# Decoder trunk on one core: conv taps on TensorE as three partial products of rounded operands, with a ring of 11 double tap matrices

## The chip, the cores and the metric

One core of one Trainium2 chip runs the whole program in one launch. The metric is the device time in microseconds (us); the host only lays data out. The engines are called as in the profile: PE is TensorE (its weight loads are listed as PEld), DVE is VectorE, ACT is ScalarE, POOL is GpSimd, SP issues the DMAs of the weights.

## What is computed

A trunk of two layers on 256 tokens of width 2048, all in float32. Layer 0 mixes with two convolution branches, layer 1 with attention; each layer then has an MLP and a gated embedding. The change touches only the first branch of layer 0:

```python
def conv_recurrent_mixer(hn, w_in, conv_a_w, conv_a_b, ln_a_g, ln_a_b, ...):
    u = hn @ w_in
    a_val, a_gate, xr, gr = jnp.split(u, [D_A, 2 * D_A, 2 * D_A + D_B], axis=-1)
    ya = a_val * jax.nn.sigmoid(a_gate)                      # GLU, 1024 channels
    ya = causal_depthwise_conv(ya, conv_a_w, conv_a_b)       # 31 taps for each channel
    ya = jax.nn.silu(layer_norm(ya, ln_a_g, ln_a_b))
    ...
    return jnp.concatenate([ya, yb], axis=-1) @ w_out
```

## The kernel before, in words

Every activation lies transposed in SBUF: 128 channels on the partitions, 256 tokens along the free dimension. A weight matrix comes in chunks of 512 rows by 256 columns, 812 chunks in all, through a ring of 4 raw buffers and a ring of 8 split buffers (`spl`). ACT rounds a chunk to fp32r (`split`, copy at L861), DVE or, for 12 chunks of this stretch (`SUMMED`), POOL subtracts the rounded part to get the remainder (L1337, L463), and PE multiplies three partial products: rounded by rounded, rounded by remainder, remainder by rounded. SP loads chunk m once the remainder of chunk m-4 is there; ACT splits chunk m once PE has used chunk m-8.

The GLU stretch has four pairs of channel tiles. Here chunk n means the n-th chunk from C_GLU on; pair c takes chunks 8c to 8c+3 for the values and 8c+4 to 8c+7 for the gates (`small_gemm`, L533 to L535, 24 matmuls for a chunk). After the last chunk of a pair DVE scales the gate (L1723), ACT takes its sigmoid (L1128), DVE multiplies (L1736, `glu_ready`).

The 31 taps of the convolution are shared out. Of the first tile of a pair DVE does 19 taps and POOL adds 12 products that ACT makes (`products`). Of the second tile PE does the first 14 taps (12 in the last pair) and DVE the rest. A tap on PE is one float32 matmul with a diagonal matrix of the tap's weights (L803); ACT makes the matrix from the identity (`tap_matrices`, L1174) in a ring of 22, `dg_ready` and `dg_used` counting both ways.

The order on each engine is written out by hand. On PE the taps of pair c-1 stand in three bursts (`conv`): 4 taps ahead of chunk 8c+6, 5 after chunk 8c+7, and 5 ahead of chunk 8c+10. The third burst of pair 2 comes ahead of chunk 33, where the output projection has begun with two chunks for a group, and the 12 taps of pair 3 come 3 at a time after chunks 33, 35, 37 and 39. ACT goes through `glu_pair(c)`: eight turns q, each with an eighth of the tap matrices of pair c-1, the split of chunk 8c+8+q and, from q=1 to 6, two products; then the sigmoid of pair c. At q=4 of c=1 it also rounds a tile XB of 2048 columns. So all matrices of pair c-1 are made ahead of the sigmoid of pair c. DVE goes through its own `glu_pair(c)`: taps in eight parts, remainders, `glu_value` and `conv_end(c-2)` at q=3, and at the end the gate and the multiplication. `conv_end` adds the parts of PE (L1810), DVE and POOL, and sums tiles for the layer norm; PE's `ln_mean` (L818) ahead of chunk 41 waits for the last of these sums.

Of the kernel before, what the change touches and what calls it, by code (L numbers as in the profile page):

```python
# [28 lines left out]
P = 128  # L29
D = 2048  # L30
T = 256
# [38 lines left out]
NDG = 22  # L70
# [28 lines left out]
LAM_STEPS = 17  # L99
OUT_PIECES = ((0, 2), (2, 6), (6, 11), (11, 16))  # L100
# [28 lines left out]
def trunk(nc, xT, pT, par, w_in, w_rg_a, w_rg_x, w_out, w_qkv, w_o, w_up, w_down, w_proj, w_gate, outT):  # L129
    with ExitStack() as ctx:  # L130
# [29 lines left out]
        with nc.sbuf_tensor("glu", [P, 8, PAD_A + T], F32) as glu, \  # L160
                nc.sbuf_tensor("xrp", [P, 2, XRP], F32) as xrp, \
                nc.sbuf_tensor("rest", [P, 8 * 2 * T - 8 * (PAD_A + T) - 2 * XRP], F32) as rest, \
                nc.sbuf_tensor("rg", [P, 8, 2, T], F32) as rg:
            prod = rest[:, 0:NPROD * T].rearrange("p (k n) -> p k n", k=NPROD)
# [6 lines left out]
        pp = sb("pp", [P, NT, T])  # L171

# [6 lines left out]
        with nc.sbuf_tensor("y", [P, 8, T], F32) as y, nc.sbuf_tensor("y2", [P, T], F32) as y2, \  # L179
                nc.sbuf_tensor("dg", [P, NDG, P], F32) as dg, nc.sbuf_tensor("ident", [P, P], F32) as ident:  # L180
            pass
# [57 lines left out]
        ln_sum = sem("ln_sum")  # L239
        dg_ready = sem("dg_ready")  # L240
        dg_used = sem("dg_used")
        conv_taken = sem("conv_taken")
        xr_step = sem("xr_step")
# [60 lines left out]
        def par_col(c):  # L304
            return params[:, bass.ds(c, 1)]

# [133 lines left out]
        def _(pool):  # L440
# [4 lines left out]
            pool.memset(glu[:, :, 0:PAD_A], 0.0)  # L445
            pool.memset(xrp[:, :, 0:PAD_B], 0.0)
# [38 lines left out]
        def _(pe):  # L485
# [304 lines left out]
            def conv(pair, part, parts):  # L790
# [4 lines left out]
                if part == 0:  # L795
                    pe.wait_ge(glu_ready, pair + 1)
# [3 lines left out]
                for k in range(part * n // parts, (part + 1) * n // parts):  # L800
                    tap = taps_upto(pair) + k
                    pe.wait_ge(dg_ready, tap + 1)
                    pe.matmul(O[:, pair % 2, 0:256], dg[:, tap % NDG, :], glu[:, bass.ds(pair * 2 + 1, 1), k:k + T],  # L803
                              start=(k == 0), stop=(k == n - 1), skip_group_check=True).then_inc(dg_used, 1)
# [54 lines left out]
        def _(act):  # L859
# [187 lines left out]
            act.wait_ge(par_rest, 16)  # L1047
            act.activation(small[:, 0, :], params[:, LAMBDA:LAMBDA + 8], ACT.Abs).then_inc(lam_abs, 1)
# [117 lines left out]
            def tap_matrices(pair, part, parts):  # L1166


                n = TAPS_PE[pair]
                for k in range(part * n // parts, (part + 1) * n // parts):  # L1170
                    tap = taps_upto(pair) + k
                    if tap >= NDG:
                        act.wait_ge(dg_used, tap + 1 - NDG)
                    act.activation(dg[:, tap % NDG, :], ident[:, :], ACT.Copy,  # L1174
                                   scale=par_col((pair * 2 + 1) * CA + (CONV_A_W + k))).then_inc(dg_ready, 1)
# [12 lines left out]
            def glu_pair(c):  # L1188
                for q in range(8):
                    tap_matrices(c - 1, q, 8)  # L1190
# [7 lines left out]
                glu_gate(c)  # L1198

            act.wait_ge(rg_vec, 11)  # L1200
# [24 lines left out]
            for s in range(NG):  # L1225
                if s < 4:
# [793 lines left out]
```

## Time and profile before

| | us |
|---|---|
| median of 3 runs | 2348.19 |
| lowest, highest | 2347.66, 2349.77 |
| the profiled execution, its time | 2347.8 |
| its span, first to last instruction | 2346.1 |
| busy in the span: PE, DVE, ACT, POOL | 2324.9, 1534.6, 1252.6, 77.1 |

The page gives busy time for each engine and the chain of work that ended last. The trace behind it is asked by stretch of time, by line or tile, or as a timeline. The GLU stretch runs from about 105 us to 220 us of the span, the taps on PE from 145 us to 243 us. In a timeline the duration of a matmul reaches beyond the start of the next; the distance between starts is what a matmul costs in a stream. The same holds for ACT and DVE, whose instructions overlap by about 0.1 us.

### The profile page before, as it was taken

How to read it: one execution, taken by the hardware profiler on the slowest of the kernel's cores; microseconds unless marked ns; L12 is line 12 of the kernel's file. 1: busy time of each engine (PE TensorE's matmuls, PEld its weight loads, DVE VectorE, ACT ScalarE, POOL GpSimd, SP SyncE). 2: the span in 40 equal slices, each digit the busy share in tenths (PEclk: the TensorE clock that was granted, in tenths of full speed). 3: DMA queues.
4: the chain of work that ended last, by engine and by line, in shares of the span. 5: the costliest groups of instructions: out<-in, count | busy, mean ns of one | idle time of the engine just before them, and what ended most of it. 6: DMA issues, size and time to landing. Idle time of an engine off the chain costs nothing.

```text
span 2346.1 us, 39851 instructions
## 1 busy us (share of the span) xinstructions
PE 2324.9 (99%) x13964; PEld 2078.5 (89%) x13964; DVE 1534.6 (65%) x1848; ACT 1252.6 (53%) x1616; POOL 77.1 (3%) x73
## 2 busy tenths in 40 slices
PE   8999999999999999999999999999999999999998
PEld 7999998888888888888888888888888888888887
DVE  8899776556556555668676666765555555556666
ACT  6876655445445435556666666555444444445454
POOL 0046100000000000000000000000000000000000
PEclk9999999999999999999999999999999999999999
DMA  8555465655655665665555555565556556556553
GB/s 254 181 181 161 154 206 172 195 179 190 194 189 182 191 199 179 188 205 174 186 179 157 176 170 177 180 190 179 189 196 188 180 194 198 179 184 202 186 166 122
DMA packets 432334, 431.24 MB, mean 184 GB/s; under 512 B 13312, under 2 KB 430208, under 8 KB 432256
## 3 DMA queue, kind: packets, MB, share of 16 engines
q1 hardware_dynamic: 431968, 429.97, 58.1%
q8 instruction: 49, 0.80, 0.1%
q10 hardware_dynamic: 288, 0.23, 0.0%
q14 instruction: 29, 0.24, 0.0%
HBM read 428.05 MB, written 2.10 MB: 183 GB/s over the span
## 4 chain that ended last, share of the span: by engine, by line
PE 97%; DVE 1%; ACT 1%; DMA 1%; issue 0%; DVEq 0%; ACTq 0%; SPq 0%
PE ps L492 54%; PE ps L498 28%; PE ps L533 3%; PE ps L534 3%; PE ps L535 3%; PE ps L490 2%; PE ps L497 1%; PE O L803 1%; DVE spl L1337 1%; DMA raw<-in_w_o 0%; PE O L654 0%; PE Z L628 0%; ACT spl L861 0%; PE Z L637 0%; PE ps L707 0%
## 5 line engine op out<-in xcount | busy, mean ns | idle before, releaser
L1337 DVE TENSOR_TENSOR spl<-raw,spl 128x1024 fp32r<-128x1024 f32 x797 | 938.6, 1222 | 579.5 <-ACT spl L861 572.2
L861 ACT ACTIVATE spl<-raw 128x1024 fp32r<-128x1024 f32 (+1 forms) x811 | 817.3, 1054 | 686.5 <-PE ps L498 593.7
L492 PE MATMUL ps<-XA,spl 128*128 128x512 f32 x2816 | 705.0, 392 | 7.3 <-DVE spl L1545 6.7
L492 PE MATMUL ps<-XB,spl 128*128 128x512 f32 x2784 | 711.5, 392 | 0.0
L492 PEld LDWEIGHTS ps<-XA,spl 128*128 128x128 f32 x2816 | 505.1, 189 | 91.5 <-issue 7.4
L492 PEld LDWEIGHTS ps<-XB,spl 128*128 128x128 f32 x2784 | 491.4, 188 | 75.6
L498 PEld LDWEIGHTS ps<-XB,spl 128*128 128x128 f32 x2784 | 394.5, 191 | 39.0
L498 PEld LDWEIGHTS ps<-XA,spl 128*128 128x128 f32 x2816 | 387.3, 191 | 31.4
L498 PE MATMUL ps<-XB,spl 128*128 128x256 f32 x2784 | 402.6, 281 | 0.0
L498 PE MATMUL ps<-XA,spl 128*128 128x256 f32 x2816 | 393.8, 282 | 0.0
L1373 DVE TENSOR_TENSOR tv<-cross,ps 128x512 f32<-128x512 f32 x181 | 123.2, 681 | 13.2 <-ACT cross L861 13.0
L941 ACT ACTIVATE tv<-tv 128x512 f32<-128x512 f32 x64 | 40.5, 633 | 168.8 <-DVE tv L1428 168.8
L861 ACT ACTIVATE cross<-ps 128x512 f32<-128x512 f32 (+1 forms) x184 | 106.4, 578 | 12.1 <-PE ps L498 11.9
L490 PE MATMUL ps<-spl,XB 128*128 128x512 f32 x256 | 80.7, 397 | 0.0
L533 PE MATMUL ps<-XB,spl 128*128 128x256 f32 x256 | 73.9, 289 | 0.0
L533 PE MATMUL ps<-XA,spl 128*128 128x256 f32 x256 | 73.7, 288 | 0.0
L534 PE MATMUL ps<-XA,spl 128*128 128x256 f32 x256 | 72.4, 283 | 0.0
L535 PE MATMUL ps<-XA,spl 128*128 128x256 f32 x256 | 72.4, 283 | 0.0
L534 PE MATMUL ps<-XB,spl 128*128 128x256 f32 x256 | 72.4, 283 | 0.0
L535 PE MATMUL ps<-XB,spl 128*128 128x256 f32 x256 | 72.4, 283 | 0.0
L1415 DVE TENSOR_TENSOR h<-h,tv 128x512 f32 (+1 forms) x87 | 60.3, 693 | 12.6 <-DVE tv L1373 11.3
L914 ACT ACTIVATE tv<-h 128x512 f32 (+1 forms) x47 | 29.7, 631 | 60.5 <-DVE h L1415 58.7
(207 smaller groups left out, 1531.6 us busy)
## 6 DMA issues: line engine op xcount, KB each, us to landing
raw<-in_w_up SPq DMA_DIRECT2D x256, 512.0 KB, 4.8
raw<-in_w_down SPq DMA_DIRECT2D x256, 512.0 KB, 5.2
raw<-in_w_qkv SPq DMA_DIRECT2D x96, 512.0 KB, 4.4
raw<-in_w_gate SPq DMA_DIRECT2D x64, 512.0 KB, 4.6
raw<-in_w_in SPq DMA_DIRECT2D x63, 512.0 KB, 4.7
raw<-in_w_out SPq DMA_DIRECT2D x32, 512.0 KB, 3.6
raw<-in_w_o SPq DMA_DIRECT2D x32, 512.0 KB, 4.8
raw<-in_w_proj SPq DMA_DIRECT2D x8, 512.0 KB, 4.1
```

The source lines that it names most:

```text
L490: pe.matmul(ps[:, b + o, :], x[:, kt, 0, c], w[:, q, :, :], start=start, stop=False)
L492: pe.matmul(ps[:, b + o, :], w[:, q, 0, c], x[:, kt, :, :], start=start, stop=False)
L498: return pe.matmul(ps[:, b + o, 0:256], w[:, q, 1, c], x[:, kt, 0, :], start=False, stop=stop)
L533: pe.matmul(out, w[0], x[0], start=start, stop=False, skip_group_check=True)
L534: pe.matmul(out, w[0], x[1], start=False, stop=False, skip_group_check=True)
L535: return pe.matmul(out, w[1], x[0], start=False, stop=stop, skip_group_check=True)
L861: return act.activation(out, in_, ACT.Copy, scale=scale)
L914: act.activation(tv[:, :, :], h[:, bass.ds(t0, 2), :], ACT.Square).then_inc(sq_ready, 1)
L941: act.activation(tv[:, :, :], tv[:, :, :], ACT.Square).then_inc(up_sq, 1)
L1337: dve.tensor_tensor(s[:, :, 1, :], raw[:, m % NRAW, :, :], s[:, :, 0, :].bitcast(F32), ALU.subtract).then_inc(lo_ready, 1)
L1373: dve.tensor_tensor(tv[:, :, :] if out is None else out, cross[:, :, :], ps[:, b:b + 2, 0:256], ALU.add).then_inc(sum_ready, 1)
L1415: dve.tensor_tensor(ht, ht, tv[:, :, :], ALU.add).then_inc(res_ready, 1)
```

## The change

The second tile of each GLU pair and its tap weights are rounded to fp32r and their remainders kept (`gs`, `wt`). A tap on PE becomes two fp32r matmuls in place of one float32 matmul: the rounded weights times rounded tile and remainder together (512 columns), and the weights' remainder times the rounded tile (256 columns). Two matrices are made for a tap, the ring holds 11 such pairs in the memory of the former 22, and ACT's order of making them changes. `round_glu` is new on ACT after each sigmoid, a subtraction is new on DVE after each multiplication, and `conv_end` has one addition more. The products of ACT for POOL move from `rest` to a part of `pp`.

```diff
-NDG = 22
+NDG = 11
...
+                nc.sbuf_tensor("gs", [P, 2, 2, PAD_A + T], F32R) as gs, \
+                nc.sbuf_tensor("wt", [P, 2, 4, NWT], F32R) as wt, \
...
+            pool.memset(gs[:, :, :, 0:PAD_A].bitcast(F32), 0.0)
...
                 if part == 0:
-                    pe.wait_ge(glu_ready, pair + 1)
+                    pe.wait_ge(gs_ready, pair + 1)
...
                     pe.wait_ge(dg_ready, tap + 1)
-                    pe.matmul(O[:, pair % 2, 0:256], dg[:, tap % NDG, :], glu[:, bass.ds(pair * 2 + 1, 1), k:k + T],
-                              start=(k == 0), stop=(k == n - 1), skip_group_check=True).then_inc(dg_used, 1)
+                    w = dg[:, tap % NDG, :, :]
+                    pe.matmul(O[:, pair % 2, :], w[:, 0, :], gs[:, pair % 2, :, k:k + T],
+                              start=(k == 0), stop=False, skip_group_check=True)
+                    pe.matmul(O[:, pair % 2, 0:256], w[:, 1, :], gs[:, pair % 2, 0, k:k + T],
+                              start=False, stop=(k == n - 1), skip_group_check=True).then_inc(dg_used, 1)
...
+            copy(wt[:, 0, :, :], taps_of_pe()).then_inc(wt_hi, 1)
...
-            def tap_matrices(pair, part, parts):
-
-
-                n = TAPS_PE[pair]
-                for k in range(part * n // parts, (part + 1) * n // parts):
+            def tap_matrices(pair, k0, k1):
+
+
+                for k in range(k0, k1):
                     tap = taps_upto(pair) + k
                     if tap >= NDG:
                         act.wait_ge(dg_used, tap + 1 - NDG)
-                    act.activation(dg[:, tap % NDG, :], ident[:, :], ACT.Copy,
-                                   scale=par_col((pair * 2 + 1) * CA + (CONV_A_W + k))).then_inc(dg_ready, 1)
+                    for j in range(2):
+                        r = act.activation(dg[:, tap % NDG, j, :], ident[:, :], ACT.Copy,
+                                           scale=wt[:, j, pair, k:k + 1].bitcast(F32))
+                    r.then_inc(dg_ready, 1)
+
+            def round_glu(pair):
+
+                if pair >= 2:
+                    act.wait_ge(conv_taken, pair - 1)
+                act.wait_ge(glu_ready, pair + 1)
+                copy(gs[:, pair % 2, 0, PAD_A:], glu[:, 2 * pair + 1, PAD_A:]).then_inc(gs_hi, 1)
...
             def glu_pair(c):
                 for q in range(8):
-                    tap_matrices(c - 1, q, 8)
+                    if q < 2 and c >= 2:
+                        tap_matrices(c - 2, TAPS_PE[c - 2] * (4 + q) // 6, TAPS_PE[c - 2] * (5 + q) // 6)
+                    elif q >= 2:
+                        n = TAPS_PE[c - 1]
+                        cut = (0, 0, 0, n // 12, n // 6, n // 4, n // 3, n // 2, 2 * n // 3)
+                        tap_matrices(c - 1, cut[q], cut[q + 1])
                     split(C_GLU + NSPL + 8 * c + q)
...
                 glu_gate(c)
-
-            act.wait_ge(rg_vec, 11)
+                round_glu(c)
+
+            act.wait_ge(rg_vec, 12)
+            act.wait_ge(wt_ready, 1)
+            round_glu(0)
             glu_pair(1)
...
             for s in range(NG):
+                if s == 0:
+                    tap_matrices(2, TAPS_PE[2] * 4 // 6, TAPS_PE[2])
                 if s < 4:
-                    tap_matrices(3, s, 4)
+                    tap_matrices(3, s * TAPS_PE[3] // 4, (s + 1) * TAPS_PE[3] // 4)
...
+            dve.wait_ge(wt_hi, 1)
+            dve.tensor_tensor(wt[:, 1, :, :], taps_of_pe(), wt[:, 0, :, :].bitcast(F32),
+                              ALU.subtract).then_inc(wt_ready, 1)
...
                 dve.wait_ge(glu_ready, c + 1)
+                dve.wait_ge(gs_hi, c + 1)
+                dve.tensor_tensor(gs[:, c % 2, 1, PAD_A:], glu[:, 2 * c + 1, PAD_A:],
+                                  gs[:, c % 2, 0, PAD_A:].bitcast(F32), ALU.subtract).then_inc(gs_ready, 1)
...
-                dve.tensor_tensor(second, second, O[:, pair % 2, 0:256], ALU.add).then_inc(conv_taken, 1)
+                for j in range(2):
+                    dve.tensor_tensor(second, second, O[:, pair % 2, j * T:(j + 1) * T], ALU.add).then_inc(
+                        (conv_half, conv_taken)[j], 1)
+                    if j == 0:
+                        dve.wait_ge(conv_half, pair + 1)
```

## Rows read from the trace of the kernel before

**Rows 1.** The page: busy time of PE, and the chain that ended last by engine

```profile
PE 2324.9 (99%) x13964; PEld 2078.5 (89%) x13964; DVE 1534.6 (65%) x1848; ACT 1252.6 (53%) x1616; POOL 77.1 (3%) x73
...
PE 97%; DVE 1%; ACT 1%; DMA 1%; issue 0%; DVEq 0%; ACTq 0%; SPq 0%
```

**Rows 2.** Stretches: length; busy us of PE, PEld, DVE, ACT, POOL; PEclk; DMA share; GB/s

```profile
138.00:163.00 25.00, 25.00 (x188) 24.25 (x188) 24.24 (x44) 19.37 (x36) 19.91 (x14) 1.00 0.68 209
...
214.00:248.00 34.00, 32.31 (x244) 31.19 (x242) 31.42 (x62) 18.36 (x34) 17.45 (x14) 1.00 0.48 147
```

**Rows 3.** Timeline of PE at two bursts: start, duration, engine, line, operation

```profile
145.01 0.28 PE L535 MATMUL ps<-XA,spl 128*128 128x256 f32 x1
145.13 1.89 PE L803 MATMUL O<-glu,dg 128*128 128x256 f32 x8
146.67 0.47 PE L533 MATMUL ps<-XA,spl 128*128 128x256 f32 x1
146.98 0.28 PE L534 MATMUL ps<-XA,spl 128*128 128x256 f32 x1
...
160.54 2.33 PE L803 MATMUL O<-glu,dg 128*128 128x256 f32 x10
```

**Rows 4.** Timeline of PE in the projection before the GLU stretch

```profile
101.28 0.63 PE L492 MATMUL ps<-XA,spl 128*128 128x512 f32 x2
101.74 0.40 PE L498 MATMUL ps<-XA,spl 128*128 128x256 f32 x2
101.97 0.63 PE L492 MATMUL ps<-XA,spl 128*128 128x512 f32 x2
```

**Rows 5.** Timeline of ACT in turns of c=1, and the sigmoid that ends them

```profile
137.81 1.06 ACT L861 ACTIVATE spl<-raw 128x1024 fp32r<-128x1024 f32 x1 [0.89 <-DMA raw<-in_w_in]
...
142.50 0.68 ACT L1174 ACTIVATE dg<-ident,params 128x128 f32<-128x128 f32 x2
143.08 1.04 ACT L861 ACTIVATE spl<-raw 128x1024 fp32r<-128x1024 f32 x1
144.03 0.89 ACT L861 ACTIVATE rest<-glu,params 128x256 f32<-128x256 f32 x2
...
149.27 1.90 ACT L861 ACTIVATE XB<-pp 128x2048 fp32r<-128x2048 f32 x1
...
165.28 0.63 ACT L1128 ACTIVATE tv<-tv 128x512 f32<-128x512 f32 x1 [7.91 <-DVE tv L1723]
```

**Rows 6.** Timeline of DVE at the multiplications of pairs 0 and 1

```profile
136.00 0.69 DVE L1736 TENSOR_TENSOR glu<-glu,tv 128x512 f32<-128x512 f32 x1 [0.35 <-ACT tv L1128]
...
138.90 1.22 DVE L1337 TENSOR_TENSOR spl<-raw,spl 128x1024 fp32r<-128x1024 f32 x1 [0.65 <-ACT spl L861]
...
164.56 0.68 DVE L1723 TENSOR_TENSOR tv<-ps,rB 128x512 f32<-128x512 f32 x1
166.01 0.69 DVE L1736 TENSOR_TENSOR glu<-glu,tv 128x512 f32<-128x512 f32 x1 [0.77 <-ACT tv L1128]
```

**Rows 7.** The tile `raw` from 125 to 165 us: from issue to landing

```profile
DMA to landing us min/median/max: 3.7/4.8/6.6
```

**Rows 8.** Waits from 246 to 300 us: total, times, longest

```profile
PE Z L818 <- DVE nacc L1818: 1.7, 1, 1.7
```

**Rows 9.** Stretches at the end of the span, columns as in rows 2

```profile
2334.00:2338.00 4.00, 1.38 (x8) 1.04 (x8) 1.98 (x6) 1.71 (x4) 0.00 (x0) 0.84 0.00 0
2338.00:2346.00 8.00, 0.00 (x0) 0.00 (x0) 3.66 (x3) 0.00 (x0) 0.00 (x0) 0.50 0.77 262
```

**Rows 10.** Timeline of PE at the end of its work

```profile
2332.48 0.51 PE L717 MATMUL Z<-onesD,nacc 128*128 128x1 f32 x4
2334.99 0.61 PE L721 MATMUL Z<-onesD,tv 128*128 128x1 f32 x4 [2.00 <-DVE tv L1523]
```

**Rows 11.** Timeline of PE near the start of the span

```profile
10.65 1.05 PE L492 MATMUL ps<-XA,spl 128*128 128x512 f32 x2
...
11.94 0.76 PE L492 MATMUL ps<-XA,spl 128*128 128x512 f32 x2
```

More of the change, by code:

```diff
@@ L99 @@
 LAM_STEPS = 17
+NWT = 18
+assert 8 * 2 * T == 8 * (PAD_A + T) + 2 * XRP + 4 * (PAD_A + T) + 8 * NWT
 OUT_PIECES = ((0, 2), (2, 6), (6, 11), (11, 16))
@@ L161, in trunk @@
                 nc.sbuf_tensor("xrp", [P, 2, XRP], F32) as xrp, \
-                nc.sbuf_tensor("rest", [P, 8 * 2 * T - 8 * (PAD_A + T) - 2 * XRP], F32) as rest, \
+                nc.sbuf_tensor("gs", [P, 2, 2, PAD_A + T], F32R) as gs, \
+                nc.sbuf_tensor("wt", [P, 2, 4, NWT], F32R) as wt, \
                 nc.sbuf_tensor("rg", [P, 8, 2, T], F32) as rg:
-            prod = rest[:, 0:NPROD * T].rearrange("p (k n) -> p k n", k=NPROD)
+            pass
         XB = sb("XB", [P, NT, 2, T], F32R)
@@ L171, in trunk @@
         pp = sb("pp", [P, NT, T])
+        prod = pp[:, 8:8 + NPROD, :]
         with nc.sbuf_tensor("wrg", [P, 2, 4, 2, 256], F32R) as wrg:
@@ L179, in trunk @@
         with nc.sbuf_tensor("y", [P, 8, T], F32) as y, nc.sbuf_tensor("y2", [P, T], F32) as y2, \
-                nc.sbuf_tensor("dg", [P, NDG, P], F32) as dg, nc.sbuf_tensor("ident", [P, P], F32) as ident:
+                nc.sbuf_tensor("dg", [P, NDG, 2, P], F32R) as dg, nc.sbuf_tensor("ident", [P, P], F32) as ident:
             pass
@@ L239, in trunk @@
         ln_sum = sem("ln_sum")
+        wt_hi = sem("wt_hi")
+        wt_ready = sem("wt_ready")
+        gs_hi = sem("gs_hi")
+        gs_ready = sem("gs_ready")
         dg_ready = sem("dg_ready")
@@ L242, in trunk @@
         conv_taken = sem("conv_taken")
+        conv_half = sem("conv_half")
         xr_step = sem("xr_step")
@@ L305, in par_col, with taps_of_pe @@
             return params[:, bass.ds(c, 1)]
+        def taps_of_pe():
+            return params[:, CONV_A_W:CONV_A_W + 8 * CA].rearrange("p (c j k) -> p c j k", c=4, j=2)[:, :, 1, 0:NWT]
         def gain(n, t):
```

## The prediction

> **What bounds the kernel now.** I read the page first: PE is busy for 99% of the span and 97% of the chain [rows 1]. Second, the busy time by stretch: in the GLU stretch PE is busy throughout until 214 us, DVE too is busy for 97% (24.24 of 25.00), and ACT for 77%, before it gets new work [rows 2]. Third, the timelines of PE, ACT and DVE side by side. PE sets the end, so PE time saved or lost here reaches the end in full; DVE has almost no room, and it decides when ACT may take the sigmoid of a pair: ACT waited 7.91 us for it at c=1 [rows 5]. The last question is whether each matrix is ready when its burst begins. Before, all of them were made ahead of that sigmoid. The change puts 5 of 14 behind it.
>
> **What a tap costs on PE.** Old: between the last matmul ahead of the first burst (145.01) and the second behind it (146.98) lie 1.97 us, of which two ordinary steps are 0.24; 1.73 for 4 taps is 0.43 a tap [rows 3]. New: two matmuls of 512 and two of 256 columns took 101.97 - 101.28 = 0.69 us, so one of each 0.35 [rows 4]. 54 taps save 54 x 0.08 = 4.5 us on PE. Bounds: a spacing of 0.12 for each 256 columns, as in small_gemm (the two steps above), gives 0.36 and 3.8 us; for the other end I take 0.34 and 4.9.
>
> **What is added to ACT and DVE.** Two matrices in a row take 143.08 - 142.50 = 0.58 us, so each of 54 new ones 0.29, 15.7 us in all; a pair of products, 256 columns each, is 0.8 by starts, so round_glu is 0.45; a split 0.95 to 1.0 [rows 5]. A pair of 14 taps gives ACT 4.1 us more in some 28 us of PE, so ACT isn't overloaded. DVE gets per pair a 256-column subtraction and an addition, about 0.4 us each, and a wait for ACT's rounding. The memset of pads on POOL (0.2 us), the rounding of the tap weights on ACT and their subtraction on DVE (0.2 us each, at 25 us and later) lie beside PE's work, and before the start of the first products on POOL; if that cover were gone they would cost their 0.6 us. The products' new place costs the same. No DMA is added; but loads go out when DVE has a remainder, so DVE's delay moves SP's queue.
>
> **First stall: ahead of chunk 14.** ACT must round the GLU tile behind the split of chunk 15 (137.81 [rows 5]), so at 138.8 to 139.2, and DVE, which has multiplied by 136.7, stands until 139.3, subtracts to 139.7, and only then makes the remainders of chunks 14 and 15. Queued behind its wait are these, the taps, and with them the loads of chunks 18 and 19. The second (begun at 138.90, 1.14 by starts [rows 6]) ended at 140.0, now at 142.0: DVE is 2.0 us late. So chunk 18 is loaded from 140.9 and, by 4.5 to 4.8 us to landing [rows 7], there at 145.4; 19 at 146.9, 20 at 149.3. ACT then goes: split 16 and 17 and two products by 142.5, matrices of tap 0 by 143.1; waits for chunk 18, split 146.4, products 147.2, tap 1 by 147.8; split 19, products, tap 2 by 150.2; split 20 151.1, products 151.9, XB 153.7 (1.8 us, [rows 5]), tap 3 by 154.3. PE comes at 145.13 [rows 3] and finds tap 0; without a wait it would be done at 146.5, now at 154.7. That is 8.2 us. The old order had made the fourth matrix by 143.1.
>
> **Second stall: ahead of chunk 18.** PE: chunks 14 and 15 (24 x 0.12 = 2.88 us each) to 160.4, second burst 162.2 (tap 8 is made by 160.9), chunks 16 and 17 to 168.0. DVE: 2.0 us late, waits about 0.7 for the split of chunk 22 (ACT has three taps' matrices to make ahead of it), so its gate begins at 167.2 - 0.7 = 166.6, where it was 164.56, and the product is there at 168.75 (it was 166.70) [rows 6]. ACT: rounding to 169.25, taps 9 and 10 to 170.4, split 171.4, taps 11 to 13 to 173.1. PE ends this burst at 173.4 instead of 169.7: 3.7 us. Even with DVE no later than before it would be 166.7 + 0.5 + 1.2 + 1.0 + 1.75 + 0.35 = 171.5, where the burst that began at 160.54 [rows 3] ended at 162.7. That floor does not depend on the first stall.
>
> **Third and fourth.** From here ACT and DVE go in step with PE, which frees the chunks. Let T be the end of chunk 22. ACT has split chunk 30 at T + 1.0; DVE's remainder (1.1), its six taps (2.5), the remainder of chunk 31 (1.2) and the gate (0.7) end at T + 6.6, sigmoid T + 7.3, product T + 8.1, rounding T + 8.6, and the last of the five pairs of matrices with a split between, T + 12.5, the burst T + 12.85. PE alone would end it at T + 2.9 + 1.75 + 5.8 + 1.75 = T + 12.1: 0.7 us, I take 0.6. For pair 2 one chunk less lies in front of the burst and no split between the matrices: T + 11.8 against T + 9.25, 2.55 us. The taps of pair 3 are made in time (ahead of chunk 34 by 230.9, needed at 232.4). Then DVE waits for the split of chunk 40, which stands behind 8 pairs of matrices (4.6 us), and comes to ln_mean 3.0 us after PE, where PE had waited 1.8 (1.7 in the waits [rows 8], and 0.1 of reentry): +1.2.
>
> **The clock.** At the end of the span PE had only a few tiny matmuls from 2332.48 on and waited 2.00 us ahead of those at 2334.99 [rows 10]; the granted clock was 0.84 of 2.4 GHz in the mean of 2334 to 2338 and 0.50, the 1.2 GHz level, after it [rows 9]. In the first stall PE would run two taps, 0.7 us, in 8.8 us, much the same. I take it that the clock falls once. At the start a set of two 512 and two 256 columns took 11.94 - 10.65 = 1.29 us [rows 11], at full clock 0.69 [rows 4], and this lasted from 6.7 to 11.9: 5.3 us at half speed, a loss of 2.65. It passes through, since ACT and DVE wait for PE's chunk 14: +2.65. The Trainium skill, page "TensorE: Matmul & The Clock Gate", Part 1, says that the array falls to half clock when idle and must be kept at work for a while before it is given the full clock again, and warns against idle gaps; by it this is a cost of the change, and if it didn't hold in a gap broken by single taps, my sum would be 11.9 (the second rival).
>
> **Sum.** 8.2 + 3.7 + 0.6 + 2.55 + 1.2 + 2.65 - 4.5 = 14.4 us. The profiled execution took 2347.8 with a span of 2346.1, so 2360.5 of span and 2362.2; the median is 0.4 above that execution: 2362.6.
>
> **The rivals.**
> 1. The forecast, 2362.6. For it: the order of ACT's queue is fixed, and DVE was too late for it by 5 us before (sigmoid 165.28 against a burst at 160.54 [rows 3, 5]). Chance 0.48.
> 2. The same stalls, but the clock stays: 14.4 - 2.65, 2360.0. For it: single taps in the gap, and the first stall may be shorter if loads land at the 3.7 end [rows 7]. Chance 0.20.
> 3. ACT and DVE are less late: DVE finds its 2 us again by 164 us, the first stall is 5 us with the clock kept, and ln_mean's wait doesn't grow. Since the second stall makes up for a shorter first one, what counts is the gate: 11.75 - 2.0 - 0.7 - 1.2 = some 8, 2356. Chance 0.16.
> 4. The clock falls again, in the second stall (1.4 us idle, then one and two taps at a time) or in the fourth: 2.65 more, 2365.3. Chance 0.08.
> 5. Faster: the matrices are ready for every burst and only PE's 4.5 us count, 2343.7. It decides at one place, the matrices of taps 9 to 13 of each pair: the gate of pair 1 would have to be ready about 10 us earlier than 166.70 [rows 6], which would need DVE to run its taps in less than half the time. Its weakness is that nothing in the change takes work from DVE. Chance 0.04.
> 6. The change doesn't do what it says: matmuls on gs and dg go at the rate of float32. Then a tap costs 3 x 0.43 = 1.3 us and 54 of them 51 us more than forecast, 2414. Against it: the same type and form go at 0.35 in [rows 4]. Chance 0.02, and 0.02 for what I haven't seen.
>
> The range of 8 in 10 leaves out 4 to 6 in part: from 2355.0, rival 3 with its own play of 1 us, to 2366.5, rival 4 and a first stall 1.2 us longer. A measurement of this kernel can tell about 0.2%, 4.7 us, from no change. Faster by more than that 0.03, within it 0.05 (the edge of 5 and the best of 3), slower 0.92.
>
> **What would show it.** Right: the waits of PE name ACT's `dg` (its L1174), some 12 to 15 us in about four groups, the largest ahead of chunk 14 and ending with tap 3, just after XB's rounding; each third burst ends right after the five pairs of matrices which follow round_glu; the matmuls of taps have starts 0.35 us apart for a tap; the clock has a stretch at half speed after the first gap and PE is less than 98% busy in 145 to 235 us. Wrong: PE has no waits at bursts (then 5), a tap of more than 0.4 us (then part of the saving is gone), no fall of the clock (2), or waits at the second bursts, which I take to be in time by 0.5 us or more except the first. Outside the stretch from 138 to 262 us nothing should move but the time at which it happens.

## The result, and the profile after

| | before | after |
|---|---|---|
| median, us | 2348.98 of 6 runs | 2366.71 of 6 runs |
| lowest to highest, us | 2347.66 to 2351.10 | 2365.88 to 2369.19 |
| profiled execution, its span, us | 2347.8, 2346.1 | 2369.19, 2367.5 |

The change makes the kernel slower by 17.7 us: 1.0076 of the time before, 95% interval 1.0065 to 1.0088. The forecast was 2362.6 us with 2355.0 to 2366.5; the direction is right, the median lies 0.2 us above the range. The profiled execution of after is the longest of its six, 2.5 us above their median, and that of before lies 1.2 us under its median, so the two spans differ by 21.4 us, 3.7 more than the medians.

The page of after, busy time and the chain that ended last by engine, which answers to [rows 1]:

```profile
PE 2331.0 (98%) x13964; PEld 2080.4 (88%) x13964; DVE 1539.9 (65%) x1857; ACT 1271.7 (54%) x1675; POOL 75.0 (3%) x74
...
PE 89%; DVE 7%; ACT 2%; DMA 1%; issue 1%; SPq 0%; DVEq 0%; ACTq 0%
```

The chain now runs for 7% through DVE. The waits of after from 138 to 290 us (who waited <- for whom: us in total, times, longest):

```profile
PEld O L818 <- ACT dg L1192: 16.5, 14, 3.9
ACT tv L1146 <- DVE tv L1762: 12.5, 3, 7.3
PE O L818 <- ACT dg L1192: 12.3, 7, 3.5
...
DVE gs L1778 <- ACT gs L878: 3.4, 4, 1.6
...
PE Z L835 <- DVE nacc L1864: 2.4, 1, 2.4
```

PE waits for ACT's tap matrices, which it did not do at all before. ACT itself was never idle ahead of one of its 108 matrices, so none of them waited for a free place in the ring. The first burst on PE, which answers to the taps of [rows 3] (start, duration, then in brackets the idle time before it and what ended it):

```profile
148.49 0.40 PE L818 MATMUL O<-gs,dg 128*128 128x512 f32 x1
148.72 0.28 PE L820 MATMUL O<-gs,dg 128*128 128x256 f32 x1
149.83 0.50 PE L818 MATMUL O<-gs,dg 128*128 128x512 f32 x1 [0.83 <-ACT dg L1192]
...
152.16 0.60 PE L818 MATMUL O<-gs,dg 128*128 128x512 f32 x1 [1.71 <-ACT dg L1192]
...
156.36 0.79 PE L818 MATMUL O<-gs,dg 128*128 128x512 f32 x1 [3.39 <-ACT dg L1192]
156.95 0.41 PE L820 MATMUL O<-gs,dg 128*128 128x256 f32 x1
```

Each tap comes alone, with a growing gap ahead of it; the fourth starts 7.9 us after the first. ACT in the same stretch, and up to the second stall:

```profile
153.83 1.89 ACT L878 ACTIVATE XB<-pp 128x2048 fp32r<-128x2048 f32 x1
155.63 0.68 ACT L1192 ACTIVATE dg<-ident,wt 128x128 fp32r<-128x128 f32 x2
...
172.46 0.63 ACT L1146 ACTIVATE tv<-tv 128x512 f32<-128x512 f32 x1 [7.27 <-DVE tv L1762]
173.92 0.42 ACT L878 ACTIVATE gs<-glu 128x256 fp32r<-128x256 f32 x1 [0.83 <-DVE glu L1775]
174.24 1.26 ACT L1192 ACTIVATE dg<-ident,wt 128x128 fp32r<-128x128 f32 x4
175.41 1.04 ACT L878 ACTIVATE spl<-raw 128x1024 fp32r<-128x1024 f32 x1
176.36 1.84 ACT L1192 ACTIVATE dg<-ident,wt 128x128 fp32r<-128x128 f32 x6
```

Tap 3's pair of matrices comes right behind XB. The sigmoid waited 7.27 us for DVE's gate (7.91 before [rows 5]), and only behind it and the rounding of the tile are the matrices of taps 9 to 13 made. PE's third burst, which stands for them:

```profile
174.97 0.50 PE L818 MATMUL O<-gs,dg 128*128 128x512 f32 x1 [3.47 <-ACT dg L1192]
...
177.09 0.79 PE L818 MATMUL O<-gs,dg 128*128 128x512 f32 x1 [0.92 <-ACT dg L1192]
```

A burst of pair 1 that finds its matrices ready shows the price of a tap (last and first matmuls of the chunks around the five taps):

```profile
199.47 0.28 PE L549 MATMUL ps<-XA,spl 128*128 128x256 f32 x1
199.59 0.40 PE L818 MATMUL O<-gs,dg 128*128 128x512 f32 x1
...
201.36 0.28 PE L547 MATMUL ps<-XA,spl 128*128 128x256 f32 x1
201.47 0.28 PE L548 MATMUL ps<-XA,spl 128*128 128x256 f32 x1
```

From 199.47 to 201.47 lie 2.00 us; less two ordinary steps of 0.12, five taps took 1.76, 0.352 a tap. Last, the granted clock. The columns are the stretch and its length, busy us (instructions) of PE, PEld, DVE, ACT and POOL, the clock as a share of 2.4 GHz, the DMA share and GB/s:

```profile
145.00:152.00 7.00, 4.62 (x35) 3.98 (x33) 6.96 (x14) 5.65 (x14) 6.45 (x5) 1.00 0.83 259
152.00:159.00 7.00, 3.45 (x13) 2.85 (x14) 6.93 (x11) 7.00 (x14) 6.57 (x6) 0.53 0.56 184
159.00:176.00 17.00, 13.53 (x103) 12.67 (x101) 15.61 (x26) 7.50 (x18) 4.77 (x5) 0.99 0.39 124
176.00:183.00 7.00, 6.08 (x26) 5.62 (x25) 5.45 (x12) 4.53 (x12) 3.07 (x2) 0.52 0.29 79
183.00:268.00 85.00, 80.55 (x616) 76.59 (x616) 73.42 (x147) 62.36 (x139) 50.40 (x40) 1.00 0.46 143
268.00:272.00 4.00, 4.00 (x21) 3.95 (x21) 3.00 (x2) 0.97 (x1) 0.00 (x0) 0.57 0.46 128
```

Three stretches are at the 1.2 GHz level: one in the first stall, one right behind the second, and one behind the wait at `ln_mean`. Ahead of each PE had just stood with no or hardly any matmuls.

**Where the time went.** For every matmul which both kernels have outside the taps I took its start in after less its start in before. I call the shift just ahead of the first burst the head. It is 3.4 us here (0.7 from 9 us of the span on, 2.9 from 60, 3.3 from 103). In a second profiled execution of the same kernel (`ctl_after`, below) it is 0.8, and in the other kernels 0.5 to 2.4, so it is a variation of the start and not the change. The growth of the shift behind the head, cleared of the 0.08 us that each tap saves:

| place | summed as | after | `ctl_after` |
|---|---|---|---|
| first stall | 8.2 | 7.4 | 8.55 |
| clock, first fall | 2.65 | 0.75 | 1.5 |
| second stall | 3.7 | 6.25 | 4.35 |
| clock, second fall | none | 1.5 | 1.35 |
| third burst of pair 1 | 0.6 | 1.0 | 1.0 |
| third burst of pair 2 | 2.55 | 2.95 | 2.95 |
| `ln_mean` | 1.2 | 0.75 | 0.75 |
| clock, third fall | none | 1.45 | 1.5 |
| saving on 54 taps | -4.5 | -4.3 | -4.3 |
| sum | 14.4 | 17.8 | 17.7 |

The first three lines measure 14.4 together in both executions, though each line differs between them, and were summed as 14.55. The excess is in the falls of the clock that were not in the sum, 2.95 us, and in two stalls of 0.4 us more each, less 0.45 at `ln_mean`.

### The profile page after: what moved, and what is told of

Same layout as the page of the kernel before. It is cut to its first block, busy times and chain, and to the rows that moved or that the text cites. A ratio compares the mean times of both kernels' runs of the same rounds, so it can differ in the third digit from the quotient of the medians.

```text
span 2367.5 us, 39923 instructions
## 1 busy us (share of the span) xinstructions
PE 2331.0 (98%) x13964; PEld 2080.4 (88%) x13964; DVE 1539.9 (65%) x1857; ACT 1271.7 (54%) x1675; POOL 75.0 (3%) x74
## 4 chain that ended last, share of the span: by engine, by line
PE 89%; DVE 7%; ACT 2%; DMA 1%; issue 1%; SPq 0%; DVEq 0%; ACTq 0%
PE ps L506 51%; PE ps L512 27%; PE ps L504 2%; DVE spl L1373 2%; PE ps L547 2%; PE ps L549 2%; PE ps L548 2%; DMA raw<-in_w_in 1%; PE ps L511 1%; ACT spl L878 1%; DVE Z L1823 1%; DVE Z L1835 1%; PE O L668 0%; DVE pp L1621 0%; PE Z L642 0%
## 5 line engine op out<-in xcount | busy, mean ns | idle before, releaser
L512 PEld LDWEIGHTS ps<-XA,spl 128*128 128x128 f32 x2816 | 387.3, 191 | 31.4
```

What stands on the lines that cost most here:

```text
L512: return pe.matmul(ps[:, b + o, 0:256], w[:, q, 1, c], x[:, kt, 0, :], start=False, stop=stop)
```

## The experiments

The kernel before was timed on the same chip beside every one; its medians lie between 2348.7 and 2349.4 us. Ratios are to it, with 95% intervals.

A trace is one execution, and not always a typical one. So that traces can be compared, the table has for each kernel the head and what the stretch from there to 275 us lost against before. The last two columns are the starts of DVE's product in pairs 1 and 3, less the head (before: 166.0 and 217.0). All in us.

| kernel | median | the profiled one | head | lost in the stretch | product 1 | product 3 |
|---|---|---|---|---|---|---|
| after | 2366.71 | 2369.19 | 3.4 | 17.9 | 169.8 | 229.9 |
| `ctl_after` | 2368.57 | 2367.14 | 0.8 | 17.7 | 169.8 | 229.7 |
| `xb_later` | 2367.44 | 2367.99 | 2.2 | 18.0 | 170.5 | 229.2 |
| `f32_new_order` | 2357.22 | 2356.70 | 0.6 | 8.1 | 167.3 | 223.5 |
| `ring14b_old` | 2357.57 | 2358.15 | 1.4 | 8.9 | 169.3 | 223.7 |
| `f32_rounding` | 2355.03 | 2356.57 | 1.3 | 7.2 | 171.2 | 223.7 |
| `pool_no_rest` | 2367.79 | 2368.94 | 2.2 | 18.9 | 170.9 | 231.0 |
| `xb_later_no_rest` | 2364.81 | 2367.02 | 1.6 | 17.0 | 169.0 | 229.1 |
| `f32_rounding_no_rest` | 2352.46 | 2354.05 | 1.8 | 3.2 | 167.5 | 220.2 |
| `before_no_rest` | 2350.09 | 2350.58 | 2.0 | 0.0 | 165.3 | 217.4 |
| `f32_rounding_defer` | 2354.50 | 2353.62 | 1.4 | 4.4 | 169.7 | 222.0 |
| `ring14_defer` | 2357.44 | 2354.42 | 0.9 | 5.7 | 168.2 | 222.7 |
| `light_dve` | 2355.94 | 2354.90 | 2.4 | 3.9 | 167.8 | 221.3 |
| `more_taps` | 2356.33 | 2356.61 | 1.3 | 7.4 | 169.6 | 223.8 |
| `fillers` | 2365.01 | 2364.77 | 0.5 | 15.7 | 171.1 | 229.2 |

**1. The changed kernel again, `ctl_after`.** No edit: is what the profile of after shows the rule?

> The changed kernel once more, unchanged, as the base of the other runs. In its first profile PE came to the first burst 3.36 us later than before, most of it from loads that landed late in the first 60 us, and lost 18.0 us between there and 272 us. Theory: the 3.4 us is variation of the start and is mostly absent here, so 2366.5 (2365.5 to 2368), with the 18 us of the stretch again within 0.5. Rival: the head start is lost by the change itself, then PE again arrives at about 148.5.

2368.57 us of 4 runs, 1.0086 (1.0069 to 1.0102). Its first burst starts at 145.97, 2.5 us earlier than in the profile of after, with the same waits, and its clock is at half from 149.4 to 159.6, 173.3 to 180.1 and 265.5 to 268.9. So the three falls belong to the change, and the late start of that other execution doesn't.

**2. Shorten the first stall alone, `xb_later`.** In the first stall ACT rounds XB ahead of tap 3; one turn later it is out of the way.

```diff
-                    if c == 1 and q == 4:
+                    if c == 1 and q == 5:
```

> The change, with ACT's rounding of the 2048 columns of XB at turn 5 of c=1 in place of turn 4, so behind the matrices of tap 3. The first burst ends 1.8 us earlier. Theory (the gate sets the end of the third burst): the second stall grows by as much, total 2366.5 to 2367, no more than 0.5 us gained. Rival (stalls add up): 1.8 us faster and one fall of the clock less, 2363.5.

2367.44 us of 4 runs, 1.0078 (1.0061 to 1.0095). The first burst ran from 147.34 to 154.84, 7.5 us where it took 8.7 in after and 9.8 in its repeat. The product of pair 1, DVE's L1775, came no earlier (172.74; less the head 170.5 against 169.8), and the third burst ended at 178.7, 31.4 us after the first began (30.7 in after and in its repeat). What the first stall gave, the second took: the third burst stands behind the gate. Here the clock fell a fourth time, at 234.0 to 237.5, so how often it falls is itself not fixed.

**3. Only the order, `f32_new_order`.** The kernel before, its matmuls in float32 and single matrices, with ACT's new order and 11 places in the ring.

```diff
-NDG = 22
+NDG = 11
...
-                    tap_matrices(c - 1, q, 8)
+                    if q < 2 and c >= 2:
+                        tap_matrices(c - 2, TAPS_PE[c - 2] * (4 + q) // 6, TAPS_PE[c - 2] * (5 + q) // 6)
+                    elif q >= 2:
...
+                        tap_matrices(c - 1, cut[q], cut[q + 1])
```

> The kernel before with one part of the change alone: the float32 taps and single matrices stay, no rounding, but the ring has 11 slots and ACT makes the matrices in the order of the change. Theory (the order is the cost): taps 9 to 13 stand behind the sigmoid, whose product is at 166.7, so the third burst of pair 0 ends near 169.6 in place of 162.7, and for the later pairs some 1.3 us and one fall of the clock are added: 2348.7 + 7 to 10, 2356 to 2359. Rival (the double matrices, the rounding and DVE's wait are the cost): within 2 us of before.

2357.22 us of 6 runs, 1.0032 (1.0020 to 1.0044): 8 us for the order, with the ring of 11 that goes with it. Its waits name the same pair of engines:

```profile
ACT tv L1128 <- DVE tv L1729: 11.2, 3, 5.4
...
PE O L803 <- ACT dg L1173: 4.7, 3, 3.1
```

The time is as expected and its place is not. PE's shift grew by 5.4 us at the first burst, by 1.9 at half clock behind it (150.3 to 157.1), and by only 0.5 and 0.3 at third bursts. The expectation had put nearly all of it at the third burst of pair 0, behind the sigmoid; there PE came late already. The trace does not tell which of the two places would be enough by itself. The size of the ring changed too. Here as well ACT was never idle ahead of a matrix (54 of them), which speaks against it as a cause. The kernel that would divide order and size, 14 places with the change's order (`ring14`), gave no time, nor did a first form of the next one (`ring14_old`).

**4. Everything but the order, `ring14b_old`.** The change with 14 pairs of matrices, three of them in the unused end of `pp`, so that ACT's old order is possible.

```diff
-NDG = 11
+NDG = 14
...
-                    if q < 2 and c >= 2:
-                        tap_matrices(c - 2, TAPS_PE[c - 2] * (4 + q) // 6, TAPS_PE[c - 2] * (5 + q) // 6)
-                    elif q >= 2:
...
+                    tap_matrices(c - 1, q * n // 8, (q + 1) * n // 8)
```

> Ring of 14 double matrices (three slots in free tiles of pp), and ACT's order of before: an eighth of a pair's matrices ahead of each split, all 14 ahead of the sigmoid. Theory (order): the second, third and fourth stall go (5.9, 0.6 and 2.6 us net of savings), the clock doesn't fall there, and about 1 us of stall is left in the second burst of pair 0 behind the rounding of XB; DVE is still late at the layer norm. 2345 to 2349. Rival (ACT and DVE have too little room for 54 more matrices and the rounding, whatever the order): 2356 or more.

2357.57 us of 6 runs, 1.0034 (1.0021 to 1.0046). I had expected the gain to appear, and it did not: 9 of the 18 us went with the order, 8 stayed. The large stalls are gone. At 218 us PE is 0.8 us behind before, with a head of 1.4: of the 3.4 us that 42 taps save 0.6 is left in hand, and small waits at the bursts took the rest. Then, ahead of the first tap of pair 3:

```profile
227.05 0.77 PE L826 MATMUL O<-gs,dg 128*128 128x512 f32 x1 [5.25 <-ACT dg L1200]
```

The waits call the weight load beside it `PEld O L826 <- DVE gs L1780: 5.4, 1, 5.4`: it is the remainder of the last GLU tile. The clock went to half behind that gap, too:

```profile
214.00:224.00 10.00, 7.62 (x55) 6.68 (x54) 9.97 (x20) 5.20 (x13) 7.19 (x6) 1.00 0.53 157
224.00:231.00 7.00, 3.95 (x15) 3.69 (x16) 5.10 (x11) 5.72 (x14) 0.88 (x1) 0.51 0.24 77
```

DVE is busy for 9.97 of 10.00 us ahead of it, and its delay takes back more than PE had in hand. In PE's shift this wait makes 6.3 us and the half clock behind it 0.65. The longer wait at `ln_mean` (3.4 us, 1.7 before [rows 8]) makes 1.7, and another fall of the clock behind that (258.3 to 261.7) 1.5.

**5. Only the rounding, `f32_rounding`.** The kernel before with ACT's rounding of the GLU tile, DVE's wait and subtraction, and the products in `pp`; PE goes on with the float32 tile.

```diff
+                act.wait_ge(glu_ready, pair + 1)
+                copy(gs[:, pair % 2, 0, PAD_A:], glu[:, 2 * pair + 1, PAD_A:]).then_inc(gs_hi, 1)
...
+                dve.wait_ge(gs_hi, c + 1)
+                dve.tensor_tensor(gs[:, c % 2, 1, PAD_A:], glu[:, 2 * c + 1, PAD_A:],
+                                  gs[:, c % 2, 0, PAD_A:].bitcast(F32), ALU.subtract).then_inc(gs_ready, 1)
```

> The kernel before with another part of the change alone: ACT rounds the second GLU tile after each sigmoid and DVE waits for it and subtracts, but nothing reads the result; the taps stay float32 matmuls, with the single matrices, ring and order of before. Theory (DVE has no room in this stretch, so its added wait and work reach the end through the gate of the last pair and the layer norm): DVE is late by 2 us at pair 0 and by about 0.9 us more for each pair, minus what it waited before; 2351 to 2356, shown as waits ahead of the taps of pair 3 or the mean. Rival (DVE's additions lie beside PE's work): within 1.5 us of before.

2355.03 us of 10 runs, 1.0025 (1.0015 to 1.0034): 6 us for two instructions and a wait a pair. Again the last pair pays; of the 7.2 us that this trace lost, 5.0 are the wait ahead of pair 3's taps and 1.4 the half clock behind it (225.5 to 232.3):

```profile
ACT tv L1132 <- DVE tv L1736: 25.9, 3, 10.5
...
PEld O L807 <- DVE glu L1749: 3.8, 1, 3.8
```

The start of DVE's product in each pair, here with the head in it, shows where it falls behind (us; the spacing is the time DVE takes for a pair):

| kernel | pair 0 | 1 | 2 | 3 | spacings |
|---|---|---|---|---|---|
| before | 136.00 | 166.01 | 191.03 | 216.95 | 30.0, 25.0, 25.9 |
| f32_rounding | 137.71 | 172.51 | 198.32 | 225.09 | 34.8, 25.8, 26.8 |
| ring14b_old | 137.30 | 170.65 | 197.41 | 225.12 | 33.4, 26.8, 27.7 |
| after | 139.79 | 173.19 | 204.28 | 233.26 | 33.4, 31.1, 29.0 |

The later spacings grow by 0.8 and 0.9 in `f32_rounding`, about what the wait for ACT's rounding (0.55 and 0.6 us) and the subtraction (0.4) cost. The first grows by 4.8, more than the one wait and the one subtraction in it can make (2.0 us and 0.4).

**6. What stretches the first spacing: POOL.** In after, DVE's remainders of one chunk, and POOL's:

```profile
146.10 2.16 DVE L1373 TENSOR_TENSOR spl<-raw,spl 128x1024 fp32r<-128x1024 f32 x1
...
152.10 2.22 DVE L1373 TENSOR_TENSOR spl<-raw,spl 128x1024 fp32r<-128x1024 f32 x1
...
157.84 3.12 DVE L1373 TENSOR_TENSOR spl<-raw,spl 128x1024 fp32r<-128x1024 f32 x1
164.80 1.21 DVE L1373 TENSOR_TENSOR spl<-raw,spl 128x1024 fp32r<-128x1024 f32 x1
```

```profile
144.76 2.41 POOL L477 TENSOR_TENSOR spl<-raw,spl 128x1024 fp32r<-128x1024 f32 x1 [141.88 <-ACT spl L878]
...
150.87 2.37 POOL L477 TENSOR_TENSOR spl<-raw,spl 128x1024 fp32r<-128x1024 f32 x1 [0.26 <-ACT spl L878]
...
157.48 2.39 POOL L477 TENSOR_TENSOR spl<-raw,spl 128x1024 fp32r<-128x1024 f32 x1
```

A subtraction that starts on DVE while POOL's is under way overlaps it by 1.07, 1.14 and 2.03 us, and is longer than 1.22 by 0.94, 1.0 and 1.9. Four kernels test what that costs. In all of them POOL leaves out its 12 remainders and only marks the chunk as done, which takes a part of the computation away. The chunk is also marked earlier, so SP may load the next one sooner: the edit takes away the clash, and a little more.

```diff
-                pool.tensor_tensor(w[:, :, 1, :], raw[:, m % NRAW, :, :], w[:, :, 0, :].bitcast(F32),
-                                   ALU.subtract).then_inc(lo_summed[m % NSPL], 16)
+                pool.memset(w[:, 0, 1, 0:1].bitcast(F32), 0.0).then_inc(lo_summed[m % NSPL], 16)
```

After with this edit, `pool_no_rest`:

> The change, but POOL doesn't subtract the remainders of its 12 chunks; it clears one column and signals. The remainders of these chunks are left out. Theory (DVE and POOL share a way to SBUF): DVE's remainders at 146.10, 152.10 and 157.84, which took 2.16, 2.22 and 3.12 us while POOL subtracted, take 1.22 again, the gate of pair 1 comes 2 to 3.8 us earlier, and the second stall shrinks by as much: 2362.5 to 2365. Rival (DVE is slow there for another reason, its reading of tiles that ACT just wrote): the three stay above 2 us and the time stays at 2366.7 to 2368.

2367.79 us of 4 runs, 1.0074 (1.0058 to 1.0089): nothing. Up to pair 1's product all remainders of DVE took 1.21 to 1.23 us, and yet the product stayed at 173.15 (less the head 170.9, in after 169.8). DVE and ACT of this kernel say why:

```profile
164.19 1.23 DVE L1372 TENSOR_TENSOR spl<-raw,spl 128x1024 fp32r<-128x1024 f32 x1 [4.06 <-ACT spl L877]
```

```profile
163.09 1.06 ACT L877 ACTIVATE spl<-raw 128x1024 fp32r<-128x1024 f32 x1 [2.55 <-PE ps L548]
```

DVE, now early, waits for a split; the split waits for PE to free a buffer, and PE is late from its own first stall, which with the half clock behind it took 10.9 us of PE's shift here (7.9 in after, 9.8 in its repeat). My reading was that two ways of nearly equal length lead to the gate. If so, both must be shortened. After with this edit and that of `xb_later` together, `xb_later_no_rest`:

> Both edits together that gained nothing alone: XB rounded behind tap 3's matrices, and POOL leaving out its 12 remainders. Theory (two ways lead to the gate of pair 1, one through DVE's slowed remainders, one through PE's late chunk 14, ACT's split of chunk 22 and DVE's wait for it, nearly equally long): only with both shortened the gate comes earlier, by 1.5 to 2.5 us, 2363 to 2366. Rival (neither matters): 2366.7 to 2368.

2364.81 us of 4 runs, 1.0065 (1.0049 to 1.0080). Its four runs, 2363.0 to 2367.0, lie mostly below the ten of the changed kernel, 2365.9 to 2369.2, but the intervals overlap. The product of pair 1 is at 170.67, less the head 169.0: 1.5 and 1.9 us earlier than with one edit alone, but only 0.8 earlier than in after and its repeat, where 1.5 to 2.5 had been expected. The stretch lost 17.0 us against 17.9 and 17.7. So both edits together give somewhat more than either alone, as two ways to one gate would have it, but less than 1 us in the trace; the reading is supported and not shown. Next the same edit in `f32_rounding`, where no stall of PE stands beside it, `f32_rounding_no_rest`:

> f32_rounding without POOL's 12 remainders, which are left out (one column is cleared instead). In f32_rounding three remainders of DVE took 3.22, 1.97 and 3.30 us in place of 1.22, 4.8 in all, in before one took 1.95. Theory (the clash of DVE and POOL is the larger part of the loss): the products of pairs 0 and 1 stand 30.5 to 31.5 us apart in place of 34.8, and the time falls by 3 to 5 us, 2350 to 2352. Rival: no gain, 2354 to 2356.

2352.46 us of 10 runs, 1.0012 (1.0003 to 1.0022), 2.6 us under `f32_rounding`; the first spacing is 30.7. The base to which this belongs is the kernel before without POOL's remainders, `before_no_rest`:

> The base of the run above: the kernel before without POOL's 12 remainders, which are left out. Theory: DVE loses only 0.7 us to the clash there, and PE waited 1.7 for the layer norm's mean, so 0.5 to 1.5 us faster than before, 2347.5 to 2348.5. Rival (POOL costs DVE more than its lengthened instructions show): 3 us or more faster.

2350.09 us of 10 runs, 1.0003 (0.9994 to 1.0012): no gain, with spacings of 29.1, 25.0 and 27.0. I read it so that before, DVE had room for the clash, and with the added work it hasn't. So of the 6 us that the rounding costs, 2.6 go with POOL's remainders. Without them it still costs 2.4 (2352.5 against 2350.1). The trace of `f32_rounding_no_rest`, 1.6 us above its median, has 3.2 of this kind: 0.75 at the second burst of pair 0, 0.4 at chunk 33, 0.5 at `ln_mean`, and 1.5 at half clock behind that (251.4 to 254.8).

**7. DVE's wait out of the way, `f32_rounding_defer` and `ring14_defer`.** DVE stands for ACT's rounding ahead of two remainders, and with them two loads. Here its wait and subtraction of pairs 0 to 2 come behind the next pair's taps, where ACT is done.

```diff
+            def rest_of_glu(c):
+                dve.wait_ge(gs_hi, c + 1)
+                dve.tensor_tensor(gs[:, c % 2, 1, PAD_A:], glu[:, 2 * c + 1, PAD_A:],
+                                  gs[:, c % 2, 0, PAD_A:].bitcast(F32), ALU.subtract).then_inc(gs_ready, 1)
...
+                if q == 1 and pair < 3:
+                    rest_of_glu(pair)
```

> f32_rounding (float32 taps, rounding of the GLU tile added, result unused) with DVE's subtraction for pairs 0 to 2 moved behind its next split and the taps of the first turn, so that DVE doesn't stand still for ACT's rounding. Theory (DVE's lateness at pair 3's gate is the cost, and its largest parts are the wait of 2 us at pair 0 and the clash with POOL that this brings): 3 to 5 us faster than f32_rounding, 2350 to 2352.5. Rival (the added operations as such): no more than 1 us faster, 2354 to 2356.

2354.50 us of 8 runs, 1.0025 (1.0014 to 1.0035): no difference that can be told from 2355.03. The first spacing is still 33.3, with remainders of 1.95 and 3.13 us; pair 3's product came 1.7 us earlier than in `f32_rounding`, less the heads. The same in `ring14b_old`:

> ring14b_old (all of the change's arithmetic, ring of 14, order of before) with DVE's subtraction moved as in f32_rounding_defer. Theory: the wait ahead of the first taps of pair 3 (5.4 us there) shrinks to 1 to 3, the clock stays up, 2352 to 2354.5; still slower than before, since DVE has 3 to 4 us more to do and PE's saving can't reach past the mean of the layer norm. Rival (the double matrices on ACT delay DVE): 2356 or more.

2357.44 us of 6 runs, 1.0032 (1.0020 to 1.0045), against 2357.57. PE was ahead of before by 0.66 us at chunk 33, although its head was 0.95 late, and then stood 5.4 us for the remainder of pair 3 (`PEld O L826 <- DVE gs L1773: 5.4, 1, 5.4`). This trace is the fastest of its six runs, 3.0 us under their median, and here too the product came 1.0 us earlier. My theory that the wait ahead of the remainders is the main cost falls with these two runs: moving it brought the last product 1.0 to 1.7 us forward and the median nowhere.

**8. Take work from DVE, `light_dve` and `more_taps`.** `ring14b_old` with the remainder of the GLU tile on POOL and the three products of a tap as three matmuls of 256 columns into one half, which spares `conv_end` its second addition.

```diff
+                if n % 3 == 0:
+                    c = n // 3
+                    pool.wait_ge(gs_hi, c + 1)
+                    pool.tensor_tensor(gs[:, c % 2, 1, PAD_A:], glu[:, 2 * c + 1, PAD_A:],
+                                       gs[:, c % 2, 0, PAD_A:].bitcast(F32), ALU.subtract).then_inc(gs_ready, 1)
...
+                    for a, b in ((0, 0), (0, 1), (1, 0)):
+                        mm = pe.matmul(O[:, pair % 2, 0:256], tap_slot(tap, a), gs[:, pair % 2, b, k:k + T],
```

> All of the change's arithmetic, with ring of 14 and the order of before, and DVE's work put back to that of before: POOL subtracts the remainder of the rounded GLU tile, and a tap is three matmuls of 256 columns into one half, so conv_end has one addition. Theory (DVE sets the time at which the layer norm's mean can be taken, and PE waited 1.7 us for it before): PE's savings of 3.8 us turn into a longer wait there, 2347.5 to 2350, equal to before. Rival (PE's saving reaches the end): 2344 to 2346.

2355.94 us of 6 runs, 1.0031 (1.0019 to 1.0044), where a time equal to that of before was expected. By chunk 33 PE had gained 2.4 us on its head, and then:

```profile
PEld O L832 <- POOL gs L487: 4.8, 1, 4.8
```

Pair 3's product came at 223.68, less the head 4.3 us later than before, where `ring14b_old` was 6.8 later. So DVE's added tile work is a part of its delay, but not all. `more_taps` also gives PE two more taps of each pair and so takes them from DVE:

```diff
-TAPS_PE = (14, 14, 14, 12)
+TAPS_PE = (16, 16, 16, 14)
```

> light_dve with 2 more taps of each pair on PE in place of DVE (16, 16, 16, 14). PE gets 8 x 0.36 = 2.9 us more, DVE 8 x 0.39 = 3.1 us less, ACT 16 matrices more. Theory (DVE bound): 3 us faster than light_dve, 2345 to 2347, faster than before. Rival (PE bound): 1 to 3 us slower than light_dve.

2356.33 us of 7 runs, 1.0031 (1.0020 to 1.0042). Eight taps fewer on DVE did not bring pair 3's product forward (225.06; less the head 2.5 us later than in `light_dve`). From 136 us to 226 us DVE waits 6.7 us in 7 places for ACT's splits (3.3 in 5 in `light_dve`, 1.0 in 2 before), so I take it that ACT, with two matrices for each tap, had become the later one; that is argued and no run divides it. What the two runs show is that no price of DVE's tile work alone explains its delay.

**9. Fill the gaps, `fillers`.** The changed kernel with matmuls whose products are thrown away or add nothing in PE's gaps: 5, 12 and 25 ahead of taps 1, 2 and 3, 25 and 5 ahead of taps 9 and 11, and 16 at `ln_mean`.

```diff
+                    for _ in range(FILL.get(tap, 0)):
+                        pe.matmul(O[:, pair % 2, 0:256], gs[:, pair % 2, 0, 0:1].broadcast_to([P, P]),
+                                  gs[:, pair % 2, 0, k:k + T], start=False, stop=False, skip_group_check=True)
```

> The change, with PE given matmuls with weights of zero in its waits: 5, 12 and 25 ahead of taps 1, 2 and 3, 25 and 5 ahead of taps 9 and 11 (they add zero to the sums), and 16 ahead of the mean of the layer norm; each lot is a little shorter than the wait it lies in. Theory: the half clock costs 3.7 us in the profile of the change (0.75, 1.5 and 1.45 after its three falls), the fillers keep it up, 2363 to 2364.5. Rival (the half clock is absorbed in the next wait): no gain, 2366.7 to 2368.

2365.01 us of 4 runs, 1.0067 (1.0051 to 1.0082), 1.7 under after and 3.6 under its repeat; the intervals overlap, the four runs are 2364.1 to 2367.0. The fills of the first stall and at `ln_mean` keep the clock whole, and in the second stall a shorter fall is left:

```profile
152.00:159.00 7.00, 6.40 (x53) 6.16 (x52) 6.93 (x10) 6.86 (x14) 6.57 (x6) 1.00 0.49 152
173.00:177.00 4.00, 3.61 (x13) 3.10 (x14) 3.78 (x8) 4.00 (x12) 0.00 (x0) 0.57 0.04 15
176.00:183.00 7.00, 7.00 (x54) 6.76 (x53) 5.41 (x13) 5.40 (x13) 4.03 (x3) 0.93 0.47 144
268.00:272.00 4.00, 4.00 (x36) 4.00 (x35) 2.46 (x4) 3.45 (x3) 0.00 (x0) 1.00 0.10 39
```

So in these traces the clock falls where PE stands or nearly stands, and stays where it is given matmuls. The stretch lost 15.7 us here, some 2 less than in after and its repeat (17.9 and 17.7). The 1.5 us behind `ln_mean` came back whole. Behind the second stall the half clock was saved too (it lay from 173.6 to 177.0, ahead of the gate), but the gate itself came 1.3 us later, for a reason that I haven't found, and only 0.4 to 0.65 us were left. That all 3.7 us come back was not right.

None of these kernels is faster than the one before.

## Why the prediction was right in sign and 4 us short

- **The price of a tap** held: 0.35 from [rows 4], 0.352 measured. Rival 6 is out. The saving is real, but it reached no end: at 218 us `ring14b_old` and `ring14_defer` had 0.6 and 1.6 of 3.4 us in hand, and gave them back at pair 3. (54 x 0.08 is 4.3 and not 4.5, and rival 2 is 11.75 and not 11.9; neither moves the forecast by more than 0.2.)
- **First stall.** Its place, its releaser and the last matrix right behind XB were as told; 7.4 us for 8.2, and 8.55 in the repeat.
- **Second stall.** Worked as 3.7 and measured as 6.25 and 4.35. What was right is the reasoning under it: the gate sets the end of the third burst. From PE's arrival at the first burst to the end of the third I had 30.9 us (173.4 + 2.65 - 145.13). Measured were 30.7 in after (179.17 - 148.49) and 30.7 in its repeat (176.63 - 145.97), and `xb_later` shortened the first burst by 1.2 us and more with no gain. The split between the first fall of the clock and the second stall was wrong, their sum was not: 2.65 lost in a stretch in which PE mostly waits anyway costs 0.75 to 1.5, and the gate then takes the rest.
- **The step that failed** is the sentence "I take it that the clock falls once". It fell three times. Rival 4, with 0.08, named the second stall as a place for another fall, at 2.65 us; it cost 1.5, and a third fall that I had nowhere, behind the wait at `ln_mean`, cost 1.45. In the repeat the two cost 1.35 and 1.5. The stretch at half was priced with a dense stream [rows 11], while only the matmuls that run in it pay. A fall ahead of a gate is absorbed by it, as the first was; one behind it passes through, and these two, 2.95 us, are most of the 3.4 that is missing between 14.4 and 17.8. `fillers` bears this out for the third fall, where 1.5 us came back; for the second it is read from the traces alone.
- **Third and fourth** were 0.4 us too small each, `ln_mean` 0.45 too large: the model in steps of chunk 22 was right to that.
- **Of two causes one was costed.** My sum had DVE's 2.0 us delay and ACT's order as one chain. The order alone costs 8 us (`f32_new_order`), the rest alone another 8 (`ring14b_old`), and the rounding in the old kernel 6. The first stall, too, is mostly the order's: 5.4 us of it and the fall of the clock are there in `f32_new_order`, where DVE waits for no rounding and isn't 2.0 us late. "Nothing in the change takes work from DVE" was the right argument against rival 5, but its condition, the matrices of taps 9 to 13, was not the one that decides. `ring14b_old` has those matrices early and is 8 us slower than before: the product of pair 3 has moved to 225.12, and `ln_mean` and two falls of the clock add to that.
- **The range** ended at rival 4 and 1.2 us. With two more falls at the price of [rows 11] it would have had to reach 2367.9, and the result is in that (the repeat, 2368.57, is not).

## What to carry to other kernels

Where PE is 99% busy and another engine is 97% busy in the same stretch, both can set the time: here PE saves 4.3 us, and two small instructions and a wait for each tile around the second engine cost 6 by themselves. For work that is moved on an in-order queue, ask which wait it now stands behind, here a sigmoid that had been 5 us late for its burst before and hurt nobody. Compare traces by what they lost behind a common point, not by absolute times: heads of 0.5 to 3.4 us lie between these. When a sum has stalls in it, price the clock at each of them, by the matmuls that follow the gap; and before a cause is removed, look for a second way of the same length to the same gate.

## What the runs showed that I had not expected

A subtraction with two tiles in SBUF on DVE does not run beside one on POOL. It takes 1.21 to 1.23 us alone, and 1.89 to 3.30 when it starts while POOL's is under way, about the overlap more. Where DVE's is first, POOL's is the longer one. Both were there in the kernel before; its DVE and then its POOL:

```profile
141.47 1.21 DVE L1337 TENSOR_TENSOR spl<-raw,spl 128x1024 fp32r<-128x1024 f32 x1
142.60 0.48 DVE L1781 SCALAR_TENSOR_TENSOR Z<-glu,params,Z 128x256 f32<-128x256 f32 x1
```

```profile
141.94 3.01 POOL L463 TENSOR_TENSOR spl<-raw,spl 128x1024 fp32r<-128x1024 f32 x1 [139.21 <-ACT spl L861]
```

POOL's took 3.01 in place of 2.4 us, 0.6 more at an overlap of 0.74. The taps of DVE behind it, with one tile in SBUF and the sum in PSUM (Z), ran beside the same instruction of POOL in their usual 0.48 us. The clash is in accord with the Trainium skill, page "SBUF — State Buffer", section "Who interferes with whom", by which a DVE instruction with two inputs in SBUF contends with a GpSimd instruction that reads SBUF and the later of the two is held up; the runs with POOL's remainders left out say what it is worth at most here: 2.6 us in `f32_rounding`, and nothing that can be measured in the kernel before or, by itself, in after.
